# One core, two-layer decoder trunk: the first MLP computed like the second, its neighbours' vectors summed earlier

## The reference

```python
mod = cs @ ada_w[layer] + ada_b[layer]             # cs = silu(c); six vectors a layer
u = h * (1 + sc) + sh
h = layer_norm(alpha * h + (1 + g) * sublayer(u), ln_g, ln_b)
# layer 0: mLSTM mixer (query, key, value, output gate, out), then MLP 0
# between: kv = modulate(h, kv_shift, kv_scale) @ w_kv, with rotary on K
# layer 1: query, windowed attention over K and V, out, then MLP 1
mlp(u) = square(relu(u @ w_up)) @ w_down           # 1024 -> 4096 -> 1024
```

## Time and profile before

| | |
|---|---|
| median of three runs | 2149.24 us (2146.18 to 2151.24) |
| the profiled execution | 2148.5 us, span 2146.8 |
| TensorE busy | 2100.7 us, 98% |
| VectorE, ScalarE, GpSimd busy | 1502.8, 882.8, 270.6 us |
| MLP 0, chunks 1 to 6 | 498.53 us |
| MLP 1, chunks 1 to 6 | 460.68 us |

### The profile page before, as it was taken

One profiled execution on the slowest core, in us unless ns is written; L12 is line 12 of the kernel. 1 busy time (PEld: TensorE's weight loads), 2 busy tenths in 40 slices (PEclk: granted clock), 3 DMA queues, 4 the chain that ended last, 5 costly groups with the idle time before them and its releaser, 6 DMA issues.

```text
span 2146.8 us, 28666 instructions
## 1 busy us (share of the span) xinstructions
PE 2100.7 (98%) x9816; PEld 1702.2 (79%) x9816; DVE 1502.8 (70%) x2343; ACT 882.8 (41%) x1529; POOL 270.6 (13%) x248
## 2 busy tenths in 40 slices
PE   6999999999999999999999999999999999999998
PEld 5888888878888888888888777678787888888886
DVE  7423666678676676776768665767788788778878
ACT  4201454162234233342337455655434434534552
POOL 0000220010010110110100023232000011011034
PEclk9999999999999999999999999999999999999999
DMA  7434643303424224224121210211345433533531
GB/s 298 137 102 126 124 94 139 126 20 120 126 69 137 97 79 137 78 83 147 34 98 72 79 30 11 79 58 42 124 182 185 162 131 137 205 114 121 195 137 79
DMA packets 77315, 242.16 MB, mean 113 GB/s; under 512 B 8417, under 2 KB 8593, under 8 KB 73649
## 3 DMA queue, kind: packets, MB, share of 16 engines
q1 hardware_dynamic: 69376, 219.18, 30.1%
q0 software_dynamic: 5088, 17.48, 3.7%
q10 hardware_dynamic: 2768, 4.41, 0.5%
HBM read 225.29 MB, written 15.76 MB: 112 GB/s over the span
## 4 chain that ended last, share of the span: by engine, by line
PE 84%; DVE 7%; DMA 4%; ACT 3%; issue 2%; POOL 1%; SPq 0%; DVEq 0%; ACTq 0%; POOLq 0%
PE ps L2670 25%; PE ps L2672 25%; PE ps L2671 25%; DMA stage<-in_stream 3%; PE ps L3135 1%; PE ps L3165 1%; PE ps L3149 1%; DVE wlo L1609 1%; ACT whi L964 1%; PE ps L2914 1%; PE ps L2773 1%; PE ps L2899 1%; DMA early_place<-in_early 1%; PE ps L2903 1%; DVE stats L1918 1%
## 5 line engine op out<-in xcount | busy, mean ns | idle before, releaser
L2672 PE MATMUL ps<-uhi,wlo 128*128 128x512 f32 x760 | 296.4, 390 | 0.0
L2670 PE MATMUL ps<-whi,uhi 128*128 128x512 f32 x704 | 287.6, 408 | 0.2 <-ACT resid L1309 0.2
L2670 PE MATMUL ps<-uhi,whi 128*128 128x512 f32 x704 | 276.3, 392 | 5.9 <-DVE wlo L1609 3.2
L2672 PE MATMUL ps<-whi,ulo 128*128 128x512 f32 x704 | 275.4, 391 | 0.0
L2671 PE MATMUL ps<-wlo,uhi 128*128 128x512 f32 x704 | 274.8, 390 | 0.0
L2671 PE MATMUL ps<-ulo,whi 128*128 128x512 f32 x704 | 274.8, 390 | 0.0
L2672 PEld LDWEIGHTS ps<-uhi,wlo 128*128 128x128 f32 x760 | 143.1, 188 | 29.8
L2670 PEld LDWEIGHTS ps<-uhi,whi 128*128 128x128 f32 x704 | 132.6, 188 | 37.0 <-DVE wlo L1609 4.6
L2670 PEld LDWEIGHTS ps<-whi,uhi 128*128 128x128 f32 x704 | 132.5, 188 | 36.6 <-issue 10.0
L2672 PEld LDWEIGHTS ps<-whi,ulo 128*128 128x128 f32 x704 | 132.2, 188 | 28.9
L2671 PEld LDWEIGHTS ps<-ulo,whi 128*128 128x128 f32 x704 | 132.5, 188 | 27.2
(11 more groups left out here) (437 smaller groups left out, 4614.6 us busy)
## 6 DMA issues: line engine op xcount, KB each, us to landing
stage<-in_stream SPq DMA_DIRECT2D x248, 512.0 KB, 3.6
hlo<-ulo_dram SPq DMA_DIRECT2D x28, 1024.0 KB, 4.8
ulo<-ulo_dram SPq DMA_DIRECT2D x20, 1024.0 KB, 5.3
w_whole<-in_stream SPq DMA_DIRECT2D x14, 512.0 KB, 5.2
aux<-in_early SPq DMA_DIRECT2D x8, 512.0 KB, 7.5
early_place<-in_early SPq DMA_DIRECT2D x8, 512.0 KB, 14.2
resid<-in_xt SPq DMA_DIRECT2D x8, 512.0 KB, 15.7
resid<-in_x POOLq DMA_DIRECT2D x8, 512.0 KB, 9.7
```

The lines of the kernel that those rows point to most:

```text
L2670: pe.matmul(dst, left_hi, right_hi, start=start, stop=False, skip_group_check=more)
L2672: return pe.matmul(dst, left_lo, right_hi, start=False, stop=stop, skip_group_check=more)
```

## The change

**MLP 0 as MLP 1.** Both call the same functions now (`mlp_through(m)` on every engine): chunks 1 to 6 with both halves as seven products, the last chunk with its up half as seven. The residual's bias row is added by GpSimd to all eight tiles in both last chunks (before: in MLP 0 VectorE all; in MLP 1 GpSimd four, VectorE four), the last four of them when the up half is through. In both chunks 0 the loads come in another order (blocks 2 to 7, block 2 first).

**The vectors.** All seven that MLP 0's chunks summed are summed earlier: beside the heads of query and key (four accumulates a head), the 16 value tiles (up to three a tile), o's second half and out (G_F1, with G_F0 after it). 62 of the loads have landing places of their own: four in free columns of `qk` (each load cut into four 1 KB pieces a partition), one in `scratch`, two in `lnrows`; at most three are in use beside the value tiles. SP's loop over loads is written out for this (`issue_order`). `sum_vector` runs ten times after SC_M0's instead of three.

**Moved.** The rotary angles (13 small VectorE operations) go into MLP 0's last chunk, before the low of P6; the preparation of blocks 96 and 97 and three modulations go between its halves (`before_tail`). The first state update of the mLSTM is a copy.

The diff at its core:

```diff
+BESIDE_QK = {6: [(SH_F0, 0, 4)], 7: [(SH_F0, 4, 8)], 8: [(SC_F0, 0, 4)], 9: [(SC_F0, 4, 8)], 10: [(SH_KV, 0, 4)],
...
+BESIDE_V = [[(SH_M1, 0, 3)], [(SH_M1, 3, 6)], [(SH_M1, 6, 8), (SC_M1, 0, 1)], [(SC_M1, 1, 4)], [(SC_M1, 4, 7)],
...
+BESIDE_O1 = {t: (G_F1, t - 4, t - 3) for t in range(4, 8)}
+BESIDE_OUT0 = {0: (G_F1, 4, 5), 1: (G_F1, 5, 6), 2: (G_F1, 6, 7), 3: (G_F1, 7, 8), 4: (G_F0, 0, 2), 5: (G_F0, 2, 4),
+               6: (G_F0, 4, 6), 7: (G_F0, 6, 8)}
...
-CHUNK_LOADS = [4, 5, 2, 3, 6, 7, 8, 9]
+CHUNK_LOADS = [2, 3, 4, 5, 6, 7]
...
+def issue_order():
+    taken = [("w", w) for w in range(6)]
+    for w in range(6, 14):
+        taken += [("w", w)] + [("ada", vec, k) for vec, first, end in BESIDE_QK[w] for k in range(first, end)]
+    for tile in range(2 * T):
+        taken += [("w", w) for w in ((14, 15) if tile == T - 1 else ())]
+        taken += [("ada", vec, k) for vec, first, end in BESIDE_V[tile] for k in range(first, end)]
+        taken += [("w", w) for w in ((7 + tile,) if tile in (T + 1, T + 2) else ())]
+    out = []
+    for x in taken:
+        if x[0] == "ada" and in_side(*x[1:]):
+            n = SIDE.index(x[1:])
+            later = [m for m in range(n + 1, len(SIDE)) if SIDE_SLOT[m] == SIDE_SLOT[n]]
+            if later:
+                out.append(("side", later[0]))
+        elif NUMBER[x] + 2 < AFTER_V:
+            out.append(("turn", NUMBER[x] + 2))
+        if x == ("w", 2):
+            out += [("side", n) for n in range(4)]
+        if x == ("w", 11):
+            out += [("side", 24), ("side", 25)]
...
+        def side_place(slot):
+            if slot < 4:
+                half, col = slot % 2, 2 * HALF - 4 * P + slot // 2 * 2 * P
+                return qk[:, 4 * half:4 * half + 4, col:col + 2 * P]
+            part = scratch[:].rearrange("p a n -> p (a n)") if slot == 4 else lnrows[:, slot - 5, :]
+            return part.rearrange("p (a n) -> p a n", a=4)
...
+            def load_side(n):
+                former = [x for x in range(n) if SIDE_SLOT[x] == SIDE_SLOT[n]]
+                if former:
+                    sp.wait_ge(side_used, former[-1] + 1)
+                elif SIDE_SLOT[n] < 4:
+                    sp.wait_ge(early_sum, K)
+                else:
+                    sp.wait_ge(gate_m, 6)
+                    sp.wait_ge(gate_v, 11)
+                    sp.wait_ge(side_used, max(x for x in range(n) if SIDE_SEM[x] == SIDE_SEM[n]) + 1)
+                dst = side_place(SIDE_SLOT[n])
+                src = stream[SIDE_BASE + n]
+                sp.dma_start(dst, src.rearrange("p (a n) -> p a n", a=4)).then_inc(side_in[SIDE_SEM[n]], 16)
+            for kind, n in issue_order():
+                if kind == "turn":
+                    load_one(n)
+                else:
+                    load_side(n)
+            load_pairs(AFTER_V, N_EARLY, 0)
...
+            def mlp_sums(m):
...
+                pool.wait_ge(group_done, first + 2)
+                pool.dma_start(lnrows[:, 1, :], consts["ln_b"][2 * m].partition_broadcast(P)).then_inc(rows_in, 16)
+                pool.wait_ge(rows_ready, (2, 5)[m])
+                pool.wait_ge(dve_evac, DVE_BEFORE[first])
+                for t in range(T):
+                    if t == T // 2:
+                        pool.wait_ge(group_done, first + 14)
+                    pool.tensor_tensor(resid[:, t, 0:D], resid[:, t, 0:D], lnrows[:, 1, :],
+                                       ALU.add).then_inc(h_by_pool, 1)
...
+            def mlp_through(m, tail, between=None):
+                mlp_chunk(m)
+                with v.Fori(0, len(SEVEN)) as i:
+                    both_chunk(m, both_start(FIRST[MLP[m]], 1), 0, i)
+                both_chunk(m, both_start(FIRST[MLP[m]], CHUNKS - 1), len(SEVEN), 0, last=True)
+                if between:
+                    between()
+                last_downs(m, tail)
...
+            def before_tail():
+                preps(96, 97)
+                modulation(2, SC_KV, SH_KV, ln=1)
+                modulation(3, SC_M1, SH_M1, ln=1)
+                modulation(4, SC_F1, SH_F1, ln=2)
+            mlp_through(0, tail_kv, between=before_tail)
...
             def sum_vector(vec):
+                total, bank = total_of(vec), SUM_BANK.get(vec, M)
                 if vec == SC_M0:
                     pe.wait_ge(early_sum, K)
+                elif in_side(vec, K - 1):
+                    pe.wait_ge(side_used, SIDE.index((vec, K - 1)) + 1)
                 else:
                     pe.wait_ge(loads_used, NUMBER["ada", vec, K - 1] + 1)
-                    pe.wait_ge(sum_read, SUM_NUMBER[vec])
+                if vec != SC_M0:
+                    pe.wait_ge(sum_read, SUM_NUMBER[vec] - (1 if vec in SUM_BANK else 0))
                 for k in range(K):
-                    last = pe.matmul(ps[:, M, k:k + 1], acc[:, k * P:(k + 1) * P], ones[:, 0:1], start=True, stop=True)
...
+            sum_vector(SH_F0)
...
-                        sum_vector(SC_F0)
+                    for vec in {1: (SC_KV,), 3: (SH_M1,), 7: (SC_M1,), 9: (G_M1,)}.get(T * nh + t, ()):
+                        sum_vector(vec)
...
+                    sum_vector(G_F1)
                 if t == 0:
```

1674 lines of the change are left out of this document (718 added, 956 removed).

## The result

The changed kernel takes **2162.28 us** (median of four, 2158.34 to 2163.51), the kernel before in the same series 2147.99 (2146.18 to 2151.24): ratio 1.0062, 95% interval 1.0043 to 1.0081. It is slower by some 14 us where 14 us less were forecast. The profiled execution of the changed kernel took 2158.34 us, the shortest of its four; against the 2148.5 of before that is +9.8, and +9.7 in the span.

The account below looks back on a forecast made before the run. TensorE, busy 98% of the span, bounds the kernel. Terms -37.9 + 0.2 + 3.8 - 1.5 - 2.8 + 12.6 + 10.7 = -14.9 on 2148.5, plus 0.7 to the median, give 2134.3 us; range 2120 to 2147, leaving out 2 in 10.

Parts of the forecast that it names:

- Middle chunks, -37.9: First MLP's chunks 1 to 6: fall from 498.53 us to the second MLP's 460.68, bounds -41 to -33.
- The price of 3.2 for filling the rings: First seven-product chunk of the first MLP: 79.46 us where the other five average 76.2, some 3.2 lost.
- Chunks 0: Both MLPs' first chunks: -1.5 us in the first without sums' quarters, -2.8 in the second with w2 loaded first.
- The wait of 2.75: Second MLP's chunk 0: TensorE's wait at 1527.16 for w2's low goes as w2 loads first, -2.8 us.
- Seven sums, +12.6: Seven more vector sums on TensorE, 1.8 us each, with no idle time to hide them: +12.6.
- The first MLP's last chunk, +0.2: Fewer matmuls -5.4, loss as in the second MLP +1.1, TensorE's wait between halves +4.5; range -4.3 to +3 us.
- the strict rule: First MLP's last chunk: port lock lets all four GpSimd additions pass before modulations end, wait 6 us instead of 4.5.
- Query and key, +1.4: TensorE's wait at 59.19 for ScalarE's scratch copy, delayed by four side loads ahead of w5: +1.4 us (0 to 5).
- Values and join to o, +1.2: Between values and o: one more accumulate and one more sum stand before the lows, +1.2 us (0 to 2).
- the landing places bound the value tiles: Value tiles: side loads landing in 8.4 us cost 15, the whole gain; beyond that slower than before, chance 0.06.
- The later joins, +8.1 for three: New waits at o's second half +1.9, out's first half +2.0 and out's second half +4.2 us.
- The second MLP's last chunk, +3.8: Final rows' loads queue behind GpSimd's additions, delaying VectorE's scaling and the fifth group's evacuation: +3.8 us (0 to 7).

Follow-up runs that it names:

- five moves: Changed kernel with angles sooner, additions alternating with normalization steps, first side loads sooner, decay rows and mask held, final rows ahead: 2136.17 us, 0.9941 of the kernel before.

## Why the prediction was wrong, point by point

- **Middle chunks, -37.9: right.** They took 459.22, -39.3; the second MLP's six take 457.8 in the same profile. The price of 3.2 for filling the rings in the first of them did not come: it lost 1.8 (78.0 for 76.2), with TensorE busy throughout, and the half clock behind a wait of 2.0 that ends at 600.80 (0.74 in the window 600:604, shown at the end) accounts for nearly all of it.
- **Chunks 0: right to a microsecond in the first MLP** (-0.9 for -1.5), **short in the second.** To its chunk 0's end the change is -5.4 for -2.8. The wait of 2.75 went as forecast; the step priced it without what followed it, for 1528 to 1532 ran at 0.57 in the kernel before (12 matmuls where 17 or 18 fit), some 1.7 us. Another 1.7 isn't the change's: the kernel before also ran at 0.57 from 1364 to 1368, behind a wait of 3.1 us, and the changed kernel had the same wait at 1.00. That the new order of loads also takes the 2.8 of its first seven-product chunk was missed: the step took 79.46 for a property of the chunk, but it went when the order of the loads changed.
- **Seven sums, +12.6: right.** Leaving out seven eighths of them gave 10.2 of 11.0, and eight of the ten sums of the changed kernel last 1.70 to 1.81 from their start to the next matmul; the two in the join ran at half clock in part (2.2 and 2.5).
- **The first MLP's last chunk, +0.2: wrong by 12.7, the step that failed worst.** The sentence "the angles fall into a stretch where VectorE has waits of its own" priced them at nothing. It held the wrong thing against them: VectorE's free time, not GpSimd's additions of four tiles in that same stretch, which the prediction had in hand (12.55 us for four) but only set against the operations between the halves. Moving the angles ahead of the additions gave 8.1. The other wait was foreseen with its place and mechanism, at 4.5; it measured 6.4, the 6 of the strict rule. The rule of the Trainium skill's "SBUF — State Buffer" ("SBUF: two separate sides") was right there, and the "one or two additions pass in that time" that I took off was not. What is left, some 2 for each of the two, fits the clock: 6.4 + (6.4 - 4.5) + 2 x 2.1 = 12.5.
- **Query and key, +1.4: wrong by 7.0.** The place and the wait were named, and even the upper bound (5) covered only the wait. "Most of the delay falls into that wait" is what failed: ScalarE's waits for w5 and w6 grew from 3.9 together to 7.3, its split of w6 came 3.4 later, and TensorE waited 3.3. Then 3.4 were lost at half clock, and some 1.7 more from 116 to 121 (mean 0.66), behind a vector's sum: 3.3 + 3.4 + 1.7 - 1.4 = 7.0. Issuing the four loads two blocks sooner gave 6.6.
- **Values and join to o, +1.2: wrong by 13.7.** TensorE's wait at the end of the values is 7.2 (0.8 before); the join behind it lost some 4.9 to a mean clock of 0.67, its two sums taking 2.2 and 2.5 in place of 1.8, and waited 1.1 for an accumulate; 168 to 172 ran at 0.57, another 1.7. Of 6.4 + 4.9 + 1.1 + 1.7 = 14.1 the forecast had 1.2. The rival "the landing places bound the value tiles" had the right stage with the wrong mechanism: it asked for a landing of 8.4 us over all tiles. They landed in 4.0 to 4.6 (medians), and the tiles kept their pace but for the last two, where GpSimd's loads in 512-byte pieces were in flight. The 8.7 of the earlier trace rows stood in the prediction as that load's own time; what it does to loads beside it was not asked, though the 6.9 us of the `stage` load at 211.67 stood in the same trace.
- **The later joins, +8.1 for three and a sum of 1.8: right in sum** (+8.4 for 9.9).
- **The second MLP's last chunk, +3.8: right** (2.7 of wait, and the last chunk and the end 3.0 longer; the wait went when the rows were issued sooner).
- The forecast time itself can be had: with five moves and all the work in place the kernel takes 2136.17, 1.9 over it. But the kernel predicted was the one without them. The failure was of pricing at zero what was hidden "in a stretch with waits" without asking which other engine is busy there, and of pricing waits at their length alone.

What stays open: how much of each wait's price is the clock was read from windows, not measured by itself, and no experiment held the clock while it removed a wait; and what would part the loads at the end of the values for good (fewer bytes beside the last two tiles, or rows in larger pieces) wasn't tried.

## What to carry to other kernels

When an operation is moved under a cover, look up what all engines do there, not only the one it runs on: an addition on GpSimd turned 0.2 us operations into 2.3 us ones, however small they were. A wait of the busiest engine is to be priced with what may follow it: here the four longest new waits cost some 2 to 5 us more each at half clock, and what followed them differed from one execution to the next. And loads that are added to a stage meet its rare ones: ask not only for the mean landing time but for what the slowest load of the stage does to those beside it.
